# Where the split combinations of weight rows and of x are made in a two-layer fp32 decoder trunk

## Chip, cores and metric

The kernel runs on one core of one Trainium2 chip. The metric is the device time of one execution, in microseconds (us). Before the change the median of three runs is 2373.53 us (2373.14 to 2376.24).

## What is computed

The input x is 1024 tokens by 1024 features in fp32. Layer 0 is an mLSTM mixer, layer 1 attends in a window of 128 tokens to one shared K/V; each layer ends in a SwiGLU FFN of width 2816. Cut to what matters here:

```python
for l in range(2):
    x = x + mixer_l(rmsnorm(x, norm[l]))     # its last step is y @ w_out, y and w_out 1024 x 1024
    x = x + swiglu(rmsnorm(x, ffn_norm[l]), w_gate_up[l], w_down[l])
    if l == 0:
        k2, v2 = shared_kv(x, kv_norm, w_kv, b_kv)
return rmsnorm(x, final_norm)

def swiglu(x, w_gate_up, w_down):            # 1024 x 5632 and 2816 x 1024
    g, u = jnp.split(x @ w_gate_up, 2, axis=-1)
    return (jax.nn.silu(g) * u) @ w_down
```

## The kernel before, in words

**Seven products for eight.** Three matrix products of each layer, called out (y @ w_out), up (x @ w_gate_up) and down (hidden @ w_down), are made by a scheme with seven block products q = 0 to 6 in place of eight (`NQ = 7`). Each product needs one combination of the left blocks and one of the right blocks. Three of the seven are plain blocks, four are sums or differences (`SUM_A`, `SUM_B`). Every operand is then split in a high part (ScalarE, ACT, copies it to fp32r) and a low part (the source less the high part), and one product is three matmuls: high by high, high by low, low by high (L1939, L1940, L1941). A pair of split operands for one q is called a form here.

**Two sides.** The side that streams, `mats`, is remade for every item: sums by GpSimd (POOL, L918 to L923), high parts by ACT (L1100), low parts by VectorE (DVE, L1428) for plain q and by POOL (L928) for sums. The resident side, `forms`, has four slots of seven forms in SBUF, each form `[128, 2, 512]` fp32. In out and down a slot holds a row, that is 256 rows of w_out or w_down; in up the four slots hold the four quarters of the normed x.

**Items.** PE's work in a layer is a list of items, each seven products over `width` slots: 8 out items of width 2 (two chunks of two rows, four groups of tokens each), 22 up items of width 4 (one for each pair of 128 gate and 128 up columns), 16 down items (chunks of 3, 3, 3 and 2 rows of w_down, four groups each). Counted from the start of the layer they are items 0 to 7, 8 to 29 and 30 to 45. After each product of out or down DVE adds a 128x512 block of PSUM to X (L1446), and product 2 waits until the bank of product 0 is read, so an item is not quite free of DVE. PE, ACT, DVE and POOL each run a fixed program through the items, q by q, and wait for each other by semaphores; all loads and stores of this part are in SP's program, in order.

**Row forms.** Rows are loaded raw from w_out or w_down (1 MB each). Their four sums are made by POOL (`row_sum`, L900), their seven high parts by ACT (`row_hi`, L1090) and low parts by DVE (`row_lo`, L1422), inside the out and down items that precede their use. The first two rows of out and of down are made within item 0 and item 30 (`cold`), one row in item 29, the others one row in an item (`forms_after`).

**Seams.** The last chunk of out and of down is also a seam: as each group of X is done, ACT squares it (L1105), DVE scales the sum (L1476), POOL takes the power (L935), DVE norms the rows (L1488, for norm 2 L1485), and PE transposes them in the next item (L1957, L1968). For out the transposed group is split at once into the seven forms of its quarter (`quarter_hi`, `quarter_lo`: ACT L1116 and L1125, DVE L1498 to L1520, POOL L943). After item 7 the last quarter is transposed and split; then item 8 begins. X (4 MB) is parked in DRAM during the up part but for two tiles, its place being used for hidden blocks and raw rows, and is read back around items 29 and 30 (`x_reload`).

**Around the run.** Before layer 0's items lie four heads of the mLSTM (`head`), with the projections as plain three-pass products; after the last one DVE scales it and PE transposes it, and DVE gates it (`gate_head`) after item 0. PE's item 1 waits for that. Before layer 1's items lie the K/V and query projections and the attention steps.

Of the kernel before, what the change touches and what calls it, by code (L numbers as in the profile page):

```python
# [33 lines left out]
ALU = mybir.AluOpType  # L34
# [74 lines left out]
PLAIN_B = {0: (0, 0), 3: (1, 0), 5: (1, 1)}  # L109
SUM_B = {1: 0, 2: 1, 4: 2, 6: 3}  # L110


class Resident:


    def __init__(self, index, layer, part, number, slot):
        self.index, self.layer, self.part, self.number, self.slot = index, layer, part, number, slot
        self.slot_free_n = None
        self.before_in_raw = None
        self.before_in_sums = None  # L120


class Item:


    def __init__(self, n, kind, layer, width):
        self.n, self.kind, self.layer, self.width = n, kind, layer, width
        self.up = kind == "up"
        self.cold = False
        self.opens_chunk = False  # L130
        self.seam = None
        self.group = None
        self.rows = ()


class Unit:


    def __init__(self, base, turn=0):
# [4 lines left out]
        self.slot = base % RING  # L144
# [7 lines left out]
def yoco_kernel(nc, x, a_norm, a_w_in, a_b_gates, a_head_norm, a_w_out, kv_norm, w_kv, b_kv,  # L152
# [30 lines left out]
    forms_made, sums_made = [], []  # L183
    for l in range(2):
# [12 lines left out]
        out_rows = [add_row("out", p, p) for p in range(4)]  # L197
        for c in range(2):
            for g in range(4):
                it = add_item("out", 2)  # L200
                it.rows, it.group = out_rows[2 * c:2 * c + 2], g
                it.cold, it.opens_chunk = c == 0 and g == 0, g == 0
                it.seam = (1 + 2 * l, g) if c == 1 else None
# [5 lines left out]
        chunks = [down_rows[0:3], down_rows[3:6], down_rows[6:9], down_rows[9:11]]  # L209
        for c, chunk in enumerate(chunks):  # L210
            for i, g in enumerate((1, 2, 3, 0) if c == 0 else (0, 1, 2, 3)):
                it = add_item("down", len(chunk))
                it.rows, it.group, it.chunk = chunk, g, c
                it.cold, it.opens_chunk = c == 0 and i == 0, i == 0
                it.seam = (2 + 2 * l, i) if c == 3 else None
        for p, r in enumerate(down_rows):
            if p < 3:
                r.slot_free_n = last_up
            elif p == 3:
                r.slot_free_n = last_up  # L220
            else:
                r.slot_free_n = last_up + 4 * ((p - 4) // 3 + 1)
        p = down_rows
        out_rows[3].before_in_raw = out_rows[2]
        out_rows[3].before_in_sums = out_rows[2]
        p[1].before_in_sums = out_rows[3]
        p[2].before_in_sums = p[0]
        p[3].before_in_sums = p[1]
        for k in range(4, FP):
            p[k].before_in_raw = p[k].before_in_sums = p[k - 1]  # L230


        forms_made += [(r, q) for q in range(NQ) for r in out_rows[:2]]
        sums_made += [(r, k) for k in range(4) for r in out_rows[:2]]
        for r in out_rows[2:] + p[:1]:
            forms_made += [(r, q) for q in range(NQ)]
            sums_made += [(r, k) for k in range(4)]
        forms_made += [(r, q) for q in range(NQ) for r in p[1:3]]
        sums_made += [(r, k) for k in range(4) for r in p[1:3]]
        for r in p[3:]:  # L240
            forms_made += [(r, q) for q in range(NQ)]
            sums_made += [(r, k) for k in range(4)]

    form_no = {(r.index, q): i + 1 for i, (r, q) in enumerate(forms_made)}
    sum_no = {(r.index, k): i + 1 for i, (r, k) in enumerate(sums_made)}


    def forms_after(it, q):

        rr, i = run_rows[it.layer], it.n - runs[it.layer][0].n  # L250
        if it.cold and q < NQ:
            pair = rr[0:2] if it.kind == "out" else rr[5:7]
            return [(r, f) for f in ((0, 1, 2) if q < 0 else (q + 3,) if q < 4 else ()) for r in pair]
        if it.kind == "out":
            return [(rr[i], q)] if i in (2, 3) and q >= 0 else []
        if it.up:
            return [(rr[4], q)] if it.tile == FT - 1 and q >= 0 else []
        i -= 8 + FT
        c, g = i // 4, i % 4
        if c < 3 and g == 1 and q >= 0:  # L260
            return [(rr[4 + 3 * c + 3], q)]
        if c < 3 and g == 3 and q >= 0:
            return [(rr[4 + 3 * c + 4], q)]
        if c in (1, 2) and g == 0:
            third = rr[4 + 3 * c + 2]
            return [(third, f) for f in {-1: (0, 1, 2), 0: (3, 4), 1: (5, 6)}.get(q, ())]
        return []


    def refill_after(it, q):  # L270

        nxt = items[it.n + 1] if it.n + 1 < len(items) else None
        if nxt is None or nxt.layer != it.layer:
            return []
        if it.cold:
            return {5: [0, 1, 2], 6: [3, 4, 5, 6]}.get(q, [])
        if it.width == 2 and nxt.width == 4:
            return {1: [0], 3: [1], 5: [2]}.get(q, [])
        return [q]


    def refill_needs(it, q):

        before = items[it.n - 1]
        return NQ * before.n + (min(2 * q + 1, 6) if before.width == 2 and it.width == 4 else q) + 1
# [6 lines left out]
    seam_act = {1: 0, 2: 32, 3: 48}  # L292
    seam_dve = {1: 0, 2: 28, 3: 44}
    seam_pool = {1: 0, 3: 16}
    last_of_run = [runs[l][-1] for l in range(2)]
    sums_before = {0: {}, 1: {}}
    for l in range(2):
        r = run_rows[l]
# [1908 lines left out]
```

## Time and profile before

| | |
|---|---|
| median of the runs | 2373.53 us |
| the profiled execution | 2370.56 us, its span 2368.9 us |
| PE busy in the span | 2120.7 us (90%) |
| granted TensorE clock, mean | 0.946 |
| DMA traffic | 191.60 MB, mean 81 GB/s |

A window row gives a stretch of the span in us from its start, its length, the busy time of each engine with the count of its instructions, the granted clock as a share of full speed, the mean busy share of the 16 DMA engines and what they moved. Windows below begin where the first matmul of an item begins.

### The profile page before, as it was taken

To read this page: it belongs to the slowest core of one execution; us is meant where nothing else is said; L and a number is where in the kernel's file an instruction comes from. 1 tells how busy PE (TensorE), PEld (TensorE's weight loads), DVE (VectorE), ACT (ScalarE), POOL (GpSimd) and SP (SyncE) were. 2 spreads that over 40 slices of the span, in tenths; PEclk is the share of its full clock that TensorE was granted. 3 is DMA by queue.
4 is the path that set the end of the run, shared out by engine and by line. 5 is a ranking of instruction groups with operands and counts; after the bars stand their busy time and mean duration, and the time that the engine had idled before them with its cause. 6 is when DMAs were issued, how large, how long until landed. Compare 5 with 4: busy or idle time off the path is not lost.

```text
span 2368.9 us, 28393 instructions
## 1 busy us (share of the span) xinstructions
PE 2120.7 (90%) x9816; PEld 1731.4 (73%) x9816; DVE 1247.1 (53%) x2030; ACT 903.4 (38%) x1929; POOL 1271.5 (54%) x1009
## 2 busy tenths in 40 slices
PE   7999997659999999788979999875999999978896
PEld 6898895548888888566757777654788888857675
DVE  7433326753333334777764767776333333376775
ACT  5323323443333334333332544433433333333332
POOL 4222024766765555777736002376665666567873
PEclk9999999979999999899988999697999999989998
DMA  4222213213333222422212003122322222342222
GB/s 126 81 81 63 62 53 134 88 54 98 88 92 87 80 81 85 150 81 89 67 36 63 19 19 90 36 81 71 98 81 80 81 80 83 97 141 87 97 76 80
DMA packets 230867, 191.60 MB, mean 81 GB/s; under 512 B 31032, under 2 KB 209224, under 8 KB 230736
## 3 DMA queue, kind: packets, MB, share of 16 engines
q1 hardware_dynamic: 221824, 177.82, 25.1%
q10 hardware_dynamic: 7488, 7.34, 0.9%
q0 software_dynamic: 1424, 4.77, 0.6%
q8 instruction: 73, 1.20, 0.2%
q14 instruction: 58, 0.48, 0.1%
HBM read 147.93 MB, written 41.98 MB: 80 GB/s over the span
## 4 chain that ended last, share of the span: by engine, by line
PE 73%; DVE 12%; POOL 6%; issue 4%; ACT 4%; DMA 1%; SPq 0%; ACTq 0%; POOLq 0%; DVEq 0%
PE ps L1939 17%; PE ps L1940 17%; PE ps L1941 17%; PE ps L1840 7%; DVE forms L1422 4%; PE ps L1842 3%; DVE X L1446 2%; PE ps L2140 2%; POOL mats L928 1%; PE ps L2175 1%; PE ps L2177 1%; PE ps L2037 1%; PE ps L2036 1%; PE ps L2033 1%; POOL sum_b_s L900 1%
## 5 line engine op out<-in xcount | busy, mean ns | idle before, releaser
L1939 PE MATMUL ps<-forms,mats 128*128 128x512 f32 x2072 | 839.3, 405 | 167.9 <-DVE X L1446 110.1
L1940 PE MATMUL ps<-forms,mats 128*128 128x512 f32 x2072 | 827.5, 399 | 0.0
L1941 PE MATMUL ps<-forms,mats 128*128 128x512 f32 x2072 | 825.9, 399 | 0.0
L928 POOL TENSOR_TENSOR mats<-sum_a,mats 128x512 fp32r<-128x512 f32 (+2 forms) x368 | 425.6, 1164 | 473.8 <-ACT mats L1100 473.4
L1939 PEld LDWEIGHTS ps<-forms,mats 128*128 128x128 f32 x2072 | 402.0, 194 | 282.1 <-issue 178.0
L1941 PEld LDWEIGHTS ps<-forms,mats 128*128 128x128 f32 x2072 | 401.7, 194 | 87.0
L1940 PEld LDWEIGHTS ps<-forms,mats 128*128 128x128 f32 x2072 | 402.9, 194 | 82.2
L1100 ACT ACTIVATE mats<-sum_a 128x512 fp32r<-128x512 f32 (+2 forms) x368 | 199.9, 545 | 420.1 <-PE ps L1941 374.6
L1446 DVE TENSOR_TENSOR X<-ps,X 128x512 f32<-128x512 f32 x336 | 229.4, 685 | 158.2 <-PE ps L1941 158.0
L1428 DVE TENSOR_TENSOR mats<-stream_raw,mats 128x512 fp32r<-128x512 f32 (+2 forms) x276 | 248.1, 900 | 55.8 <-ACT mats L1100 54.5
L1100 ACT ACTIVATE mats<-stream_raw 128x512 fp32r<-128x512 f32 (+2 forms) x276 | 150.1, 544 | 284.6 <-PE ps L1941 247.8
L918 POOL TENSOR_TENSOR sum_a<-stream_raw 128x512 f32<-128x512 f32 (+2 forms) x92 | 104.6, 1137 | 262.8 <-DMA stream_raw<-scratch_y 187.9
L1840 PE MATMUL ps<-xT_hi,w_split 128*128 128x512 f32 x432 | 182.8, 423 | 3.1 <-issue 3.0
L1840 PE MATMUL ps<-xT_lo,w_split 128*128 128x512 f32 x432 | 170.7, 395 | 0.0
L1457 DVE TENSOR_TENSOR part<-ps,part 128x512 f32<-128x512 f32 x44 | 30.4, 692 | 257.6 <-PE ps L1941 257.4
L1842 PE MATMUL ps<-xT_hi,w_split 128*128 128x512 f32 x432 | 136.6, 395 | 0.0
L919 POOL TENSOR_TENSOR sum_a<-stream_raw 128x512 f32<-128x512 f32 (+2 forms) x92 | 130.5, 1419 | 0.0
L921 POOL TENSOR_TENSOR sum_a<-sum_a,stream_raw 128x512 f32<-128x512 f32 (+2 forms) x92 | 126.7, 1377 | 0.0
L1422 DVE TENSOR_TENSOR forms<-sum_b_s,forms 128x512 fp32r<-128x512 f32 x88 | 101.5, 1154 | 44.8 <-ACT forms L1090 44.2
L923 POOL TENSOR_TENSOR sum_a<-stream_raw,sum_a 128x512 f32<-128x512 f32 (+2 forms) x92 | 116.8, 1270 | 7.2
L868 POOL TENSOR_TENSOR raw<-raw,gain_cols 128x1024 f32<-128x1024 f32 x35 | 76.8, 2211 | 61.6 <-DMA raw<-in_a_w_in_dram 45.0
L1840 PEld LDWEIGHTS ps<-xT_hi,w_split 128*128 128x128 f32 x432 | 82.1, 190 | 33.6 <-issue 17.6
(216 smaller groups left out, 2715.0 us busy)
## 6 DMA issues: line engine op xcount, KB each, us to landing
stream_raw<-in_w_gate_up_dram SPq DMA_DIRECT2D x88, 512.0 KB, 5.2
scratch_hidden<-hidden SPq DMA_DIRECT2D x88, 256.0 KB, 5.3
stream_raw<-scratch_hidden SPq DMA_DIRECT2D x24, 768.0 KB, 4.8
resident_raw_e<-in_w_down_dram SPq DMA_DIRECT2D x32, 512.0 KB, 3.5
raw<-in_a_w_in_dram SPq DMA_DIRECT2D x24, 512.0 KB, 4.0
stream_raw<-scratch_y SPq DMA_DIRECT2D x16, 512.0 KB, 5.0
scratch_x<-X SPq DMA_DIRECT2D x12, 512.0 KB, 3.6
resident_raw_down<-in_w_down_dram SPq DMA_DIRECT2D x12, 512.0 KB, 5.3
```

Of the source, the lines that this page charges most:

```text
L919: pool.tensor_tensor(s[2], a11, a21, ALU.subtract)
L921: pool.tensor_tensor(s[1], s[0], a11, ALU.subtract).then_inc(ssum, 2)
L928: pool.tensor_tensor(blocks(m[:, q, 1, :], it.width), stream_source(it, q), blocks(m[:, q, 0, :].bitcast(F32), it.width), ALU.subtract).th ...
L1100: act.activation(blocks(mats[w][:, q, 0, :], w), stream_source(it, q), ACT.Copy).then_inc(hi_s, 1)
L1422: dve.tensor_tensor(forms[:, r.slot, q, 1, :], row_source(r, q), forms[:, r.slot, q, 0, :].bitcast(F32), ALU.subtract).then_inc(rlo, 1)
L1428: dve.tensor_tensor(blocks(m[:, q, 1, :], it.width), stream_source(it, q), blocks(m[:, q, 0, :].bitcast(F32), it.width), ALU.subtract).the ...
L1446: dve.tensor_tensor(xv, ps[:, s + BANK_OF[q], :], xv, ALU.add).then_inc(d_add, 1)
L1840: ms_ = [mm(ps[:, b + half, :], ah, t[:, c[half]], start=start and t is bh, stop=False) for half in halves for t in (bh, bl)]
L1842: ms_ += [mm(ps[:, b + half, :], al, bh[:, c[half]], start=False, stop=stop) for half in halves]
L1939: mm(dst, ah, bh, start=OPENS[q] and k == 0, stop=False, skip_group_check=True)
L1940: mm(dst, ah, bl, start=False, stop=False, skip_group_check=True)
L1941: m = mm(dst, al, bh, start=False, stop=k == w - 1, skip_group_check=True)
```

## The change

- Layer 0's four rows of w_out are split into forms one in each head: POOL makes four sums, ACT the high parts between its copies of v (`head_row_hi`), POOL the low parts, and POOL stores each form (512 KB) in a DRAM scratch, `scr_w` (`head_row`).
- The eleven rows of w_down of each layer, and in layer 0 also the four rows of w_out of layer 1, are split during up items 9 to 27 (`prep_rows`): in layer 0 105 forms over 133 steps (19 items of seven), in layer 1 77. POOL makes the sums, ACT the high part, DVE the low part, SP stores. There are two output buffers, so the high part of form k waits until form k-2 has landed in DRAM.
- Out and down items make no row forms. A row's seven forms are read from `scr_w`, issued on ACT's queue (the first two of each out part on SP's), as the products that used the slot before are done (`load_form`).
- Down has five chunks of 2, 3, 2, 2 and 2 rows, so 20 items a layer, with as many matmuls as before.
- In the seams ACT norms (`x_normed_of`), POOL scales and takes the power. For out the transposed tiles are only written to `xt` by DVE with the norm's gain (`evacuate`); the combinations for all four quarters are made after item 7, as item 8 needs them: POOL sums and low parts for two quarters, DVE for the other two, ACT all high parts.
- All eight tiles of X are parked. The streamed forms of item 0 are made in the last head and the last attention steps, and `gate_head` runs before item 0.

```diff
-        chunks = [down_rows[0:3], down_rows[3:6], down_rows[6:9], down_rows[9:11]]
-        for c, chunk in enumerate(chunks):
+        for c, width in enumerate((2, 3, 2, 2, 2)):
...
+        for r, at_item, free in zip(down_rows, (29, 29, 30, 31, 33, 34, 37, 38, 39, 42, 43),
+                                    (29, 29, 29, 29, 33, 33, 37, 37, 37, 41, 41)):
+            r.load_at, r.slot_free_n = at_item, runs[l][free].n
+        preps[l] += down_rows
+        if l == 1:
+            preps[0] += out_rows
...
+        events = [(runs[l][8 + f].n, q) for f in range(1, 20) for q in range(NQ)]
+        j0, forms_here = preps[l][0].prep, NQ * len(preps[l])
+        for k in range(forms_here):
+            prep_at.setdefault(events[k * len(events) // forms_here], []).append((j0 + k // NQ, k % NQ))
...
+            eng.dma_start(forms[:, r.slot, q].bitcast(F32), scr_w[r.layer, r.index % (4 + FP), q]).then_inc(row_in[q], 16)
...
+            def store_prep(j, q):
+                r, k = prep_rows[j], NQ * j + q
+                sp.wait_ge(prep_lo, k + 1)
+                sp.dma_start(scr_w[r.layer, r.index % (4 + FP), q], prep_out[k % 2][:].bitcast(F32)).then_inc(prep_stored[k % 2], 16)
...
                     if 9 <= i <= 30:
                         store_hidden(its[i - 1])
+                    if it.up:
+                        for q in range(NQ):
+                            for j, form in prep_at.get((it.n, q), []):
+                                store_prep(j, form)
+                                if form == NQ - 1 and j + 2 < end_prep:
+                                    load_prep(j + 2)
+                    if i == 28:
+                        for b in range(2):
+                            sp.wait_ge(prep_stored[b], staged(NQ * end_prep - 1, b))
+                        for t in (1, 5, 2, 6, 3, 7, 4):
+                            sp.dma_start(X[:, t, :], scr_x[l, t]).then_inc(x_back, 16)
...
+            def prep_hi_of(j, q):
+                k = NQ * j + q
+                if q in FORM_SUM:
+                    act.wait_ge(prep_sum, 4 * j + FORM_SUM[q])
+                else:
+                    act.wait_ge(prep_loaded[j % 2], raw_prep_at[j])
+                if k >= 2:
+                    act.wait_ge(prep_stored[k % 2], 16 * (k // 2))
+                act.activation(prep_out[k % 2][:, 0, :], split_source(prep_raw[j % 2], prep_t, q), ACT.Copy
+                               ).then_inc(prep_hi, 1)
...
+            def x_form_hi(l, q):
+                for c, g in enumerate(QUARTERS):
...
+                    act.activation(quarter(g, q, 0), x_form_source(g, q), ACT.Copy).then_inc(xf_hi, 1)
...
+            def x_form_lo(l, q):
+                for c, g in enumerate((2, 3)):
+                    pool.wait_ge(xf_hi, 28 * l + 4 * q + c + 1)
+                    pool.tensor_tensor(quarter(g, q, 1), x_form_source(g, q), quarter(g, q, 0).bitcast(F32),
+                                       ALU.subtract).then_inc(xf_lo_pool, 1)
...
                     if i == 7:
-                        quarter_lo(it.seam[0], 3, (0, 1, 2, 3))
-                        for q2 in (4, 5):
-                            stream_lo(its[i + 1], q2)
+                        for q in range(NQ):
+                            if q in SUM_B:
+                                x_form_sums(l, q)
+                            x_form_lo(l, q)
+                            if q in (3, 6):
+                                stream_lo(its[8], 4 if q == 3 else 5)
...
+            def x_normed_of(norm, i, t, e):
+                act.wait_ge(rstd_ready, norm * TT + 2 * i + e + 1)
...
+                act.activation((xp if norm == 2 else xn)[e][:], X[:, t, :], ACT.Copy, scale=rstd[:, t:t + 1]
+                               ).then_inc(xs_ready, 1)
...
-                    pe.wait_ge(rlo, max(form_no[r.index, q] for r in it.rows))
+                    pe.wait_ge(row_in[q], 16 * (it.rows[-1].index + 1))
                 if it.up and it.tile == 0:
...
+                    for done in (xf_lo_dve, xf_lo_pool):
+                        pe.wait_ge(done, 14 * l + 2 * q + 2)
```

## Rows read from the trace of the kernel before

**Rows 1.** The page's busy times over the whole span.
```profile
PE 2120.7 (90%) x9816; PEld 1731.4 (73%) x9816; DVE 1247.1 (53%) x2030; ACT 903.4 (38%) x1929; POOL 1271.5 (54%) x1009
```
**Rows 2.** Windows of layer 0: items 0-3, 4-7, 8, 9-28, 29, 30-45, after.
```profile
core 0: us, PE busy (x) PEld busy (x) DVE busy (x) ACT busy (x) POOL busy (x), PEclk, DMA share, GB/s
371.49:433.20 61.71, 45.23 (x171) 33.69 (x169) 49.49 (x69) 24.28 (x55) 44.48 (x43) 0.91 0.34 113
433.20:508.65 75.45, 50.98 (x213) 39.78 (x211) 48.06 (x69) 27.28 (x57) 46.43 (x45) 0.84 0.25 77
508.65:549.95 41.30, 26.25 (x106) 20.97 (x105) 17.71 (x24) 20.01 (x34) 26.78 (x21) 0.79 0.26 89
549.95:930.75 380.80, 380.80 (x1682) 315.31 (x1680) 134.25 (x160) 142.92 (x240) 234.73 (x165) 1.00 0.29 83
930.75:957.53 26.78, 19.20 (x86) 15.61 (x84) 19.76 (x21) 14.11 (x27) 15.15 (x13) 0.90 0.35 109
957.53:1227.40 269.87, 233.93 (x964) 184.72 (x964) 187.29 (x246) 98.23 (x193) 190.43 (x162) 0.94 0.27 88
1227.40:1245.00 17.60, 5.09 (x25) 3.95 (x25) 13.32 (x14) 7.48 (x13) 7.29 (x6) 0.64 0.07 30
```
**Rows 3.** Windows of layer 1: items 0-3, 4-7, 8, 29, 30-41, 42-45.
```profile
1512.42:1567.38 54.96, 43.70 (x169) 33.12 (x170) 47.33 (x65) 24.95 (x56) 44.97 (x44) 0.94 0.21 60
1567.38:1644.93 77.55, 53.08 (x213) 41.35 (x211) 47.92 (x69) 27.29 (x57) 46.34 (x45) 0.82 0.24 75
1644.93:1684.80 39.87, 24.85 (x107) 19.90 (x106) 17.93 (x24) 20.12 (x34) 27.25 (x21) 0.83 0.27 93
2065.59:2092.37 26.78, 19.20 (x85) 15.61 (x84) 19.76 (x21) 14.10 (x27) 15.14 (x13) 0.94 0.34 107
2092.37:2302.63 210.26, 186.00 (x756) 146.95 (x757) 152.60 (x185) 76.66 (x147) 167.30 (x133) 0.94 0.30 101
2302.63:2360.80 58.17, 44.83 (x169) 35.03 (x167) 32.79 (x52) 16.64 (x36) 26.37 (x30) 0.88 0.23 82
```
**Rows 4.** Windows of one item each, of width 4, 3 and 2, without row forms.
```profile
588.03:607.07 19.04, 19.04 (x85) 15.77 (x84) 7.24 (x8) 7.14 (x12) 16.89 (x13) 1.00 0.29 83
1070.34:1084.62 14.28, 14.28 (x64) 11.82 (x63) 7.83 (x11) 4.20 (x8) 9.84 (x10) 1.00 0.29 92
1528.55:1538.90 10.35, 9.80 (x43) 7.81 (x42) 7.07 (x11) 2.93 (x7) 5.17 (x8) 1.00 0.00 0
```
**Rows 5.** A window in which the DMA engines are never idle.
```profile
372.00:378.00 6.00, 3.53 (x15) 2.46 (x14) 6.00 (x8) 6.00 (x15) 5.02 (x6) 0.99 1.02 411
```
**Rows 6.** PE's waits in 371.5:523.6: who for whom, total us, times, longest.
```profile
PE ps L1939 <- DVE X L1446: 33.0, 12, 8.1
PE ps L1957 <- DVE x_normed_b L1488: 9.8, 1, 9.8
```
**Rows 7.** Groups: line engine op, names, shapes, count | busy us, mean ns | idle before.
```profile
L943 POOL TENSOR_TENSOR forms<-sum_x,forms 128x512 fp32r<-128x512 f32 x12 | 18.1, 1532 | 6.1 <-ACT forms L1125 6.1
L900 POOL TENSOR_TENSOR sum_b_s<-resident_raw_e,sum_b_s 128x512 f32<-128x512 f32 x16 | 24.4, 1526 | 1.4 <-POOL sum_b_s L900 1.4
L928 POOL TENSOR_TENSOR mats<-sum_a,mats 128x512 fp32r<-128x512 f32 x64 | 82.8, 1295 | 111.8 <-ACT mats L1100 111.8
L1422 DVE TENSOR_TENSOR forms<-sum_b_s,forms 128x512 fp32r<-128x512 f32 x36 | 41.9, 1163 | 19.8 <-ACT forms L1090 19.5
L1100 ACT ACTIVATE mats<-sum_a 128x512 fp32r<-128x512 f32 x64 | 40.2, 628 | 56.1 <-PE ps L1941 56.1
```
**Rows 8.** The timeline of DVE between norm 2 and the K/V projection.
```profile
1231.45 5.87 DVE L1485 TENSOR_SCALAR x_plain_a<-X,rstd 128x1024 f32<-128x1024 f32 x1
```
**Rows 9.** DMA issues: median us from issue to landing, of 512 KB each.
```profile
out_dram<-x_out SPq DMA_DIRECT2D x8, 512.0 KB, 2.6
scratch_x<-X SPq DMA_DIRECT2D x12, 512.0 KB, 3.6
X<-scratch_x SPq DMA_DIRECT2D x12, 512.0 KB, 6.3
```

More of the change, by code:

```diff
@@ L225, in yoco_kernel @@
[L225 to L267, printed above, removed]
@@ L270, in refill_after, with staged, last_slot_used @@
+    def staged(k, b):
+        return 16 * ((k + 1 - b) // 2 if k >= b else 0)
+    def last_slot_used(q, before, after):
+        return max(q, min(NQ - 1, ((q + 1) * after.width - 1) // before.width))
     def refill_after(it, q):
-        nxt = items[it.n + 1] if it.n + 1 < len(items) else None
-        if nxt is None or nxt.layer != it.layer:
+        i = it.n - runs[it.layer][0].n
+        if i + 1 == len(runs[it.layer]):
             return []
-        if it.cold:
-            return {5: [0, 1, 2], 6: [3, 4, 5, 6]}.get(q, [])
@@ L277, in refill_after @@
-        if it.width == 2 and nxt.width == 4:
-            return {1: [0], 3: [1], 5: [2]}.get(q, [])
-        return [q]
+        nxt = items[it.n + 1]
+        return [s for s in range(NQ if i != 7 else 3) if last_slot_used(s, it, nxt) == q]
     def refill_needs(it, q):
         before = items[it.n - 1]
-        return NQ * before.n + (min(2 * q + 1, 6) if before.width == 2 and it.width == 4 else q) + 1
+        return NQ * before.n + last_slot_used(q, before, it) + 1
     down_no = {it.n: m for m, it in enumerate(i for i in items if not i.up)}
@@ L312, in yoco_kernel @@
         stream_arrived[it.n] = stream_total[stream_buffer(it)]
-    def row_arrived(r):
-        if r.part == "out":
-            return (16, 48)[r.layer]
-        return 16 * (r.layer + 1)
     x2 = x[0]
@@ L1014, in _ @@
             load_rows_of_head(0)
-            for j in range(6, 11):
+            load_head_row(0)
+            for j in range(6, 8):
+                gain(Unit(U_HEADS + j))
+            head_row(0)
+            for j in range(8, 11):
                 gain(Unit(U_HEADS + j))
@@ L1202, in run @@
-                    if i == 7:
-                        quarter_hi(it.seam[0], 3, range(8))
-                        act.wait_ge(s_pool, 16 * (l + 1))
-                        for q in range(3, NQ):
-                            stream_hi(its[8], q)
+                        for r in rr:
+                            if r.load_at == i:
+                                if r.part == "out":
+                                    act.wait_ge(*x_free[l])
+                                else:
+                                    act.wait_ge(prod, NQ * r.slot_free_n + q + 1)
+                                load_form(act, r, q)
@@ L1312, in head @@
                     act.wait_ge(num_ready, h * TT + c + 1)
+                    if last and c:
+                        stream_hi(items[0], c - 1)
                     if c % 4 == 3:
@@ L1711, in head @@
                         write_lo(un[4 + c // 4] + LEAD)
+                    if last and c in (3, 6):
+                        stream_lo(items[0], c - 3)
                     i = 2 * c
@@ L1742, in _ @@
             head(NH_A - 1, NH_A - 1, False, last=True)
+            stream_lo(items[0], 6)
             scale_head(NH_A - 1)
+            gate_head(NH_A - 1, last=True)
             run(0)
```

727 lines of the change are left out of this document (341 added, 386 removed).

## Prediction, made before the changed kernel had run

> **What bounds the kernel now.** I read the page's busy times first. PE is busy 90% of the span and no other engine over 54% [rows 1], so only PE's idle time and its time at a low clock can be won. The windows say where these are. In items 9 to 28 PE is never idle and the clock is 1.00: 380.8 us for 20 items, 19.04 each [rows 2, 4]. The losses lie around them. In layer 0 items 0-3 take 61.7 us with 45.2 busy, items 4-7 75.5 with 51.0, item 8 with the wait before it 41.3, item 29 26.8 where a clean one takes 19.04, and items 30-45 269.9 [rows 2]; layer 1 has the same pattern [rows 3]. PE's waits name the cause: 33.0 us in the first out part is for DVE's add to X [rows 6]. The add itself is short; it stands in DVE's queue behind low parts of row forms (1163 ns each, [rows 7]), which wait for ACT and POOL. PE's other wait, 9.8 us, is for the norm of the last group.
>
> Clean items set the floor: width 4 19.04, width 3 14.28, width 2 10.35, the last with 9.8 of PE time [rows 4]. I take 10.3 for width 2.
>
> **Out part, items 0-7.** Removed are 28 row forms, each an ACT copy of 0.63 and a DVE operation of 1.16, and 16 POOL sums of 1.53 [rows 7]. In their place come 28 reads of 512 KB. Items 0-3 become 4 x 10.3 = 41.2. Item 4 is 10.3. Items 5-7 also carry 16 transposes each, about 2.1 us of PE, and the chain of two squares, scale and power, two norms on ACT (each of the four put at 1.1, just under twice the 0.63 of a copy half as wide, [rows 7]), transposes, `evacuate` at q=3. That chain reaches PE's second set of transposes about 0.8 us late, so 9.8 + 2.1 + 0.8 = 12.7 each, 38.1 for three. Bounds: 11.9 if the chain is hidden, 16.0 if it stays as bad as in layer 1's last items, (58.17 - 10.3)/3 [rows 3]. Together 89.6. Against 61.71 + 75.45 = 137.2 in layer 0 and 132.5 in layer 1 [rows 2, 3] that is -47.6 and -42.9. The reads of rows 2 and 3 (7.3 MB, 18 us at the 411 GB/s that a full DMA share moved [rows 5]) have 41 us and are hidden; without that cover they would cost item 4 what is late.
>
> **Start of the runs.** In layer 0 the last head now ends with one more high part and low part ahead of the head's scaling: +1.0 (0 to 2). `gate_head` moved ahead costs 2.7 us of DVE before the first add, but PE's first product takes 1.4 and its wait before item 1 goes, which is inside the 61.7. In layer 1 item 0 need no longer wait for forms: -2.2.
>
> **The forms of x, before and in item 8.** This step is dearer than before. After item 7's last product the last group needs 4.9 us until POOL can begin its first low part. POOL then has 8 sums and 14 low parts at 1.53 (the means of L900 and L943, [rows 7]) and two stream low parts of 1.3 (L928): 36.3. DVE has as many at 1.16, ACT 28 x 0.63 = 17.6, both less. So POOL sets the pace, about 5.2 us a form against PE's 2.7, and the seventh product ends at 4.9 + 36.3 + 2.8 = 44.0. The sums for item 9 come only then: 2.0 more. 46.0 against 41.30 and 39.87 [rows 2, 3]: +4.7 and +6.1. Bounds: all at the 1.30 of L928, -5; all a tenth dearer than 1.53 and the last products at the low clock, +9. PE idles in half of this, so I expect the low level (1.2 GHz) in part of it, as before (clock 0.79).
>
> **Up part, items 9-28.** Here work is added beside a PE that had no idle time. Per item of layer 0: 105/19 = 5.5 forms. ACT goes from 7.1 to 10.6, DVE from 6.7 to 13.1, POOL from 11.7 [rows 2] to about 18 (3.2 sums of 1.53, and about 1.5 for more overlap with DVE). All are below 19.04, POOL barely. What can bind is the pair of buffers: two forms take a high part 0.63, a low part 1.2, a store that lands after 2.6 [rows 9], the stores of out and 0.3 of semaphores, 4.7. That is 2.76 x 4.7 = 13.0 an item. The queue also carries the item's own 1.5 MB, 0.29 x 19.04 = 5.5 us of all DMA engines [rows 4], issued in one piece ahead of the stores, and 0.8 MB of raw rows, 2.0 us, mostly in gaps. Together 18.5 to 20.5; I take 19.8. What is late: ACT waits inside `prep_hi_of`, behind it its silu, then DVE's add for q=4, which PE's q=6 needs. So +0.8 x 19 = +15 (0 to +45). Layer 1 has 4.05 forms an item, 17.0 by the same sum: hidden, +3 for what POOL is behind after item 8 (0 to +10).
>
> The Trainium skill speaks against this term. Its page DMA: Bandwidth & Descriptors (Anatomy of one DMA) gives a DMA a fixed cost of about 2.0 us, mostly the receipt of the write, and HBM as the heaviest target; 512 KB is then 3.2 us, an estimate by that page. The trace has 2.6 for the same size and direction [rows 9], so I keep 2.6. By the page the item would be 21.5 and the layer's loss 46 in place of 15.
>
> **Item 29.** Its 7.7 us over the clean item was row forms that DVE made between its last add and item 30. Both layers: 2 x (26.78 - 19.04) = -15.5. The 14 reads for item 30 are released product by product, 1 MB in 2.6 us of DMA against 2.72 of PE, and have 16 us; hidden, but just.
>
> **Down part.** Layer 0: 4 items of width 3 57.1, 13 of width 2 133.9, three with transposes 38.1: 229.1 against 269.87, -40.8. More items of width 2 cost 0.8 each against their share of a width 3 item; that is in it. Layer 1: 57.1 + 12 x 10.3 = 123.6, and the last four as before, since DVE still does norm 4 and waits for POOL there: 58.2. 238.9 against 268.43: -29.5. Bounds: 9.8 to 11.0 for width 2, +-10 a layer. The late reads (one row, 3.7 MB, 9 us, for a window of 10 or 14) stand beside products.
>
> **After layer 0.** DVE's 5.87 us of x_plain_a [rows 8] stood beside three POOL operations and held PE; ACT now does it in about 1.1: -5.
>
> **Heads.** Four times 11 POOL operations and 9 DMA issues, put at 0.6 us each, lie in POOL's idle time (46% of the span, [rows 1]); one gain of a weight comes some 2 us later. +2 (0 to 8).
>
> **Sum.** -47.6 +1.0 +4.7 = -41.9 (out, layer 0); -42.9 -2.2 +6.1 = -39.0; -15.5; -40.8; -29.5; -5: -171.7. Against it +15 +3 +2. Net -151.7. PE's idle time in the windows that shrink is about 112 + 96 = 208 us, so there is room for it. Profiled 2370.56 - 151.7 = 2218.9; the median of before lies 3.0 above its profiled execution, so I forecast 2222, own range 2200 to 2245.
>
> **Rivals.**
> - *The store ring binds (22%).* Stores land as those of scratch_x did, after 3.6 [rows 9]: 2.76 us more an item, 19 x 2.76 = 52 in layer 0, layer 1 still at the edge. 2275. For it: the up part has no idle PE time, and its queue is shared. Against it: 3.6 was seen beside other transfers, which I count apart.
> - *The chains stay (13%).* Seam items stay at 16.0 (9 x 3.3 = 30) and POOL in the forms of x runs at 1.7 with a debt to the next items (about 18). 2270. For it: POOL is the pace there in any case.
> - *Reads come late (7%).* In items 29 to 31 four rows (14.7 MB, 36 us) and X (4.2 MB, 10 us) are read within about 40 us. If they queue, items 30 to 33 lose 15 a layer: 2252.
> - *Slower (6%).* The same ring, with stores that land after 6.3, as the reads of X did [rows 9]: 3.7 us more a pair of forms, 10.2 an item in layer 0 and 7.5, less 2.0 of slack, in layer 1, so 194 + 104 = 298: 2520. It decides from a landing of about 4.7 us on (2.1 more: 110 + 42 = 152). For it: 105 MB are written and as much read that were not before. Against it: the share is 0.29, and stores add 5.5 x 1.3 us an item, to about 0.77.
> - That rows were hidden anyway and the change brings nothing (2%): the waits of [rows 6] speak against it.
>
> **Numbers.** The forecast holds 50%, the rivals as said. Range 2190 to 2285: below it needs all bounds at their good ends, above it is the slower case and the worst of the ring. About 0.2% (4.7 us) is what a measurement tells from no change. Faster 0.92, same 0.02, slower 0.06.
>
> **What would show it.** Clean windows of about 10.3 and 14.28 in out and down, with no PE wait for DVE's add beyond 0.5. Item 8 with its wait at 46, PE waiting for POOL's low parts, POOL busy throughout. Items 9 to 27 of layer 0 at 19 to 20.5 with ACT waiting for a DMA to `scratch_forms`; layer 1 at 19.04. Item 29 at 19.04. The forecast is wrong if layer 0's up items are over 21, if out and down items of width 2 are over 11.5, or if PE waits for `forms<-scratch_forms`.

## The result: faster by 2.3%, where 6.4% was forecast

The changed kernel takes 2317.78 us (median of four runs, 2316.42 to 2323.76) beside 2374.89 for the kernel before: ratio 0.9765, interval 0.9745 to 0.9784. The gain is 57 us and not 152, and the time lies outside the range of 2190 to 2285. The profiled execution has a span of 2314.9 us.

The page's busy times, to be read beside [rows 1]:

```profile
PE 2099.2 (91%) x9816; PEld 1724.1 (74%) x9816; DVE 1341.7 (58%) x2046; ACT 934.6 (40%) x2001; POOL 1330.5 (57%) x1181
DMA packets 295431, 415.02 MB, mean 179 GB/s; under 512 B 40040, under 2 KB 218232, under 8 KB 295296
```

The windows: the heads; layer 0's items 0-7, the forms of x with item 8, items 9-28, item 29, the down part, what follows it up to layer 1; then layer 1's items 0-7, forms with item 8, items 9-28 and down part. They answer to [rows 2, 3].

```profile
66.00:396.40 330.40, 309.58 (x1756) 273.72 (x1755) 119.94 (x202) 106.58 (x220) 134.10 (x118) 0.96 0.39 134
396.40:495.32 98.92, 86.50 (x386) 69.25 (x384) 54.88 (x90) 35.18 (x71) 50.24 (x70) 0.94 0.59 205
495.32:556.65 61.33, 27.94 (x101) 21.93 (x101) 44.96 (x36) 29.60 (x50) 51.80 (x38) 0.69 0.20 69
556.65:1005.26 448.61, 405.02 (x1681) 327.93 (x1680) 271.45 (x265) 196.58 (x345) 326.55 (x221) 0.95 0.69 231
1005.26:1024.30 19.04, 19.04 (x85) 15.77 (x84) 5.44 (x8) 5.86 (x12) 7.36 (x10) 1.00 0.83 305
1024.30:1253.30 229.00, 219.65 (x973) 178.66 (x971) 132.74 (x210) 77.48 (x165) 127.47 (x163) 0.99 0.58 214
1253.30:1517.75 264.45, 248.66 (x1433) 194.17 (x1432) 176.10 (x610) 121.89 (x484) 51.95 (x35) 0.96 0.21 63
1517.75:1606.00 88.25, 84.97 (x384) 68.61 (x384) 53.85 (x88) 35.12 (x71) 50.25 (x70) 0.98 0.54 185
1606.00:1666.73 60.73, 27.74 (x102) 21.64 (x101) 44.75 (x36) 29.71 (x50) 52.28 (x38) 0.69 0.20 70
1666.73:2047.53 380.80, 380.80 (x1682) 315.32 (x1681) 250.94 (x237) 184.44 (x317) 307.46 (x205) 1.00 0.67 223
2066.57:2307.10 240.53, 220.14 (x925) 179.32 (x923) 133.87 (x205) 65.65 (x147) 132.14 (x163) 0.94 0.57 212
```

Set against the terms of the forecast, in us (a stretch after less the same stretch before):

| stretch | forecast | measured | off by |
|---|---|---|---|
| heads, with the start of the run | +3 | +24.9 | +21.9 |
| out items 0-7, layer 0 | -47.6 | -38.2 | +9.4 |
| out items 0-7, layer 1 | -42.9 | -44.2 | -1.3 |
| forms of x and item 8, both layers | +10.8 | +40.9 | +30.1 |
| up items 9-28, layer 0 | +15 | +67.8 | +52.8 |
| up items 9-28, layer 1 | +3 | 0.0 | -3 |
| item 29, both layers | -15.5 | -15.5 | 0 |
| down part, layer 0 / 1 | -40.8 / -29.5 | -40.9 / -27.9 | +1.5 |
| from layer 0's last item to layer 1 | -7.2 | -20.6 | -13.4 |
| sum | -151.7 | -53.7 | +98 |

What was to be saved came. What was to cost little cost 134 us: the up part of layer 0, item 8, the heads. The waits of TensorE name each place. First those of the heads, then of 396.4 to 556.65, then of items 9 to 28 of layer 0 with ACT's own wait behind them:

```profile
PE ps L2076 <- DVE C_state L1732: 10.6, 3, 5.1
PE ps L2051 <- ACT v_one L1298: 4.9, 2, 2.9
```
```profile
PE ps L1945 <- ACT part L1161: 24.6, 1, 24.6
PE ps L1945 <- DVE X L1473: 10.2, 3, 8.7
```
```profile
PE ps L1945 <- DVE part L1487: 43.6, 18, 4.9
ACT prep_forms L1098 <- DMA scratch_forms<-prep_forms: 104.0, 39, 7.3
```

In items 9 to 28 of layer 0 TensorE is idle for 43.6 us, and busy for 405.0 where the same work took 380.8: behind many of the stalls the granted clock is at its lower level (1.2 GHz) for some microseconds. 43.6 + 24.2 is the whole 67.8. The mean clock of 0.95 accounts for some 22 of the 24.2 (0.05 x 448.6).

### The profile page after: what moved, and what is told of

Read it like the earlier page. It is cut to its first block, busy times and chain, and to the rows that moved or that the text cites. A ratio compares the mean times of both kernels' runs of the same rounds, so it can differ in the third digit from the quotient of the medians.

```text
span 2314.9 us, 29195 instructions
## 1 busy us (share of the span) xinstructions
PE 2099.2 (91%) x9816; PEld 1724.1 (74%) x9816; DVE 1341.7 (58%) x2046; ACT 934.6 (40%) x2001; POOL 1330.5 (57%) x1181
## 3 DMA queue, kind: packets, MB, share of 16 engines
q1 hardware_dynamic: 254992, 286.90, 37.9%
## 4 chain that ended last, share of the span: by engine, by line
PE 65%; DVE 11%; DMA 9%; POOL 4%; issue 4%; ACT 4%; SPq 3%; ACTq 0%; POOLq 0%; DVEq 0%
PE ps L1945 15%; PE ps L1946 15%; PE ps L1947 15%; PE ps L1848 7%; DMA scratch_forms<-prep_forms 6%; PE ps L1850 3%; DVE mats L1453 2%; DMA scratch_hidden<-hidden 2%; PE ps L2128 1%; DVE hidden L1496 1%; SPq L673 1%; DVE prep_forms L1447 1%; PE ps L2163 1%; PE ps L2165 1%; ACT prep_forms L1098 1%
## 5 line engine op out<-in xcount | busy, mean ns | idle before, releaser
L874 POOL TENSOR_TENSOR mats<-sum_a,mats 128x256 fp32r<-128x256 f32 (+2 forms) x400 | 421.2, 1057 | 469.7 <-ACT mats L1119 468.9
L1119 ACT ACTIVATE mats<-sum_a 128x256 fp32r<-128x256 f32 (+2 forms) x400 | 206.2, 517 | 315.8 <-PE ps L1947 289.9
L1453 DVE TENSOR_TENSOR mats<-stream_raw,mats 128x256 fp32r<-128x256 f32 (+2 forms) x300 | 275.1, 919 | 61.7 <-ACT mats L1119 61.1
L1119 ACT ACTIVATE mats<-stream_raw 128x256 fp32r<-128x256 f32 (+2 forms) x300 | 155.3, 518 | 277.0 <-PE ps L1947 247.1
L1447 DVE TENSOR_TENSOR prep_forms<-prep_raw,prep_forms 128x512 fp32r<-128x512 f32 x130 | 158.7, 1222 | 140.0 <-ACT prep_forms L1098 140.0
L864 POOL TENSOR_TENSOR sum_a<-stream_raw 128x256 f32<-128x256 f32 (+2 forms) x100 | 110.7, 1107 | 224.4 <-DMA stream_raw<-scratch_y 194.0
L865 POOL TENSOR_TENSOR sum_a<-stream_raw 128x256 f32<-128x256 f32 (+2 forms) x100 | 125.0, 1250 | 0.0
L869 POOL TENSOR_TENSOR sum_a<-stream_raw,sum_a 128x256 f32<-128x256 f32 (+2 forms) x100 | 116.0, 1160 | 7.8
L867 POOL TENSOR_TENSOR sum_a<-sum_a,stream_raw 128x256 f32<-128x256 f32 (+2 forms) x100 | 119.6, 1196 | 0.0
L1421 DVE TENSOR_TENSOR w_split<-raw,w_split 128x1024 fp32r<-128x1024 f32 x35 | 55.1, 1590 | 100.9 <-ACT w_split L1075 100.9
L1098 ACT ACTIVATE prep_forms<-prep_raw 128x512 fp32r<-128x512 f32 x130 | 81.1, 624 | 71.6 <-DMA scratch_forms<-prep_forms 68.2
```

The lines of the kernel that those rows point to most:

```text
L865: pool.tensor_tensor(s[2], a11, a21, ALU.subtract)
L867: pool.tensor_tensor(s[1], s[0], a11, ALU.subtract).then_inc(ssum, 2)
L874: pool.tensor_tensor(blocks(m[:, q, 1, :], it.width), stream_source(it, q), blocks(m[:, q, 0, :].bitcast(F32), it.width), ALU.subtract).th ...
L1119: act.activation(blocks(mats[w][:, q, 0, :], w), stream_source(it, q), ACT.Copy).then_inc(hi_s, 1)
L1447: dve.tensor_tensor(dst[:, 1, :], split_source(prep_raw[j % 2], prep_t, q), dst[:, 0, :].bitcast(F32), ALU.subtract).then_inc(prep_lo, 1)
L1453: dve.tensor_tensor(blocks(m[:, q, 1, :], it.width), stream_source(it, q), blocks(m[:, q, 0, :].bitcast(F32), it.width), ALU.subtract).the ...
```

## The experiments

All are the changed kernel with the edits named. Their ratios are to the kernel before, whose median beside them was 2374 to 2376 us. The places that the first four edits change hardly touch, so each is also read by its own stretch.

**1. The order on GpSimd in the heads.**

```diff
-                for j in range(LEAD + 1, LEAD + 4):
+                for j in range(LEAD + 1, LEAD + 5):
                     gain(Unit(U_HEADS + j, h))
                 head_row(h)
-                for j in range(LEAD + 4, LEAD + 1 + RING):
+                for j in range(LEAD + 5, LEAD + 1 + RING):
```
(and the same for head 0)

> The changed kernel with one edit: in each head GpSimd scales the weights of the ninth unit (unit 8 of head 0, and the like in each head) before it makes the head's seven forms and not behind them. Theory A (the order on GpSimd costs the heads their 24.9 us: gain waits behind the forms, so ScalarE's and VectorE's halves of that unit come late and TensorE waits for the state C): the waits for C (10.6 us in 3 before) go, and the heads fall from 396.4 us by 12 to 20 us, so the time is 2298 to 2306 us, ratio to the kernel before 0.968 to 0.971. Theory B (the forms' own work on the shared engines, ScalarE's copies and VectorE's operations stretched beside GpSimd, costs it, in whatever order): the heads stay at 391 to 397 us, the time at 2312 to 2319 us.

Measured: 2302.86 us, ratio 0.9704 [0.9674, 0.9734]. The start of item 0 moves from 396.4 to 383.4 us, TensorE's wait for C from 10.6 to 1.8 us. Theory A. The prediction had this step ("one gain of a weight comes some 2 us later") and did not follow it to who waits: ScalarE's and VectorE's halves of the unit, C, TensorE. Of the 24.9 us this is 13.0; 11.9 stay, of them 6.6 a wait for `v_one` in head 0.

**2. The order on ScalarE in item 8.**

```diff
                             ...
                                     stream_hi(its[8], q2)
+                            if 2 <= q <= 4:
+                                up_out(its[8], q - 2)
```
(and item 8's own three calls go)

> The changed kernel with one edit: ScalarE's three copies for item 8 (which free TensorE's products 2, 4 and 5 of that item) stand between its copies for the forms of x, behind those of forms 2, 3 and 4, and not behind all 28. Theory A (the products of item 8 were held by the order on ScalarE, 24.6 us of waiting before product 2): that wait goes, and each layer's stretch from the end of item 7 to the end of item 8 falls from 61 us to 44 to 50 us, so the time is 2292 to 2306 us. Theory B (the forms themselves are made at that pace, by GpSimd and VectorE, and the wait only moves to products 5 and 6): each stretch stays at 56 to 61 us and the time at 2308 to 2318 us.

Measured: 2311.83 us, ratio 0.9732 [0.9712, 0.9752]. The wait of 24.6 us is gone, and item 8, counted from its own first product, fell only from 50.1 and 49.5 to 48.3 and 47.1: theory B in the main. TensorE now waits product by product for the forms.

```profile
506.41:554.72 48.31, 29.82 (x85) 21.73 (x85) 37.24 (x27) 21.86 (x39) 44.56 (x29) 0.75 0.19 65
```

GpSimd (44.6 us) and VectorE (37.2) are busy together. Here lies the lesson of this stretch: the largest wait in the view was not what the time hung on.

**3. A third buffer for the high halves.**

```diff
+                sp.wait_ge(prep_hi, k + 1)
+                sp.dma_start(dst[:, 0, :], prep_h[k % 3][:].bitcast(F32)).then_inc(hi_stored[k % 3], 16)
                 sp.wait_ge(prep_lo, k + 1)
-                sp.dma_start(scr_w[...], prep_out[k % 2][:].bitcast(F32)).then_inc(prep_stored[k % 2], 16)
+                sp.dma_start(dst[:, 1, :], prep_l[k % 2][:].bitcast(F32)).then_inc(lo_stored[k % 2], 16)
```

> The changed kernel with one edit in the up part: a form's high half and low half are stored by transfers of their own (256 KB each, twice as many transfers), the high halves from three buffers and the low halves from two, and ScalarE waits only for the store of the high half three forms back. Theory A (the ring of two buffers, each held by copy, subtraction, issue and landing, sets the pace where layer 0 makes 105 forms in 19 items): layer 0's items 9 to 28 fall from 448.6 us to 381 to 400 us, layer 1's stay at 380.8, and the time is 2250 to 2272 us, ratio 0.947 to 0.957. Theory B (the bytes stored, or ScalarE's and VectorE's extra operations, set it): items 9 to 28 stay above 430 us and the time at 2300 us or more; the doubled number of transfers could even add some us.

Measured: 2301.42 us, ratio 0.9676 [0.965, 0.9703]; items 9 to 28 of layer 0 take 426.95 us, between the two theories; the time is in theory B's range. The window; then, from 577 to 965 us, DVE's and ACT's waits for the stores, and the DMA issues with their landings:

```profile
556.77:983.72 426.95, 395.06 (x1682) 320.90 (x1681) 269.97 (x265) 196.55 (x345) 326.11 (x221) 0.98 0.74 243
```
```profile
DVE prep_lo L1460 <- DMA scratch_forms<-prep_lo: 52.9, 18, 7.6
ACT prep_hi L1109 <- DMA scratch_forms<-prep_hi: 13.9, 7, 3.7
```
```profile
scratch_forms<-prep_hi SPq DMA_DIRECT2D x100, 256.0 KB, 4.4
scratch_forms<-prep_lo SPq DMA_DIRECT2D x99, 256.0 KB, 3.5
```

Half the bytes land no sooner (these are medians). ScalarE's wait fell from 104.0 us to 13.9, and VectorE took over with 52.9: the low halves still have two buffers. A whole form landed in 3.5 (median) in the changed kernel.

**4. The row loads one item later.**

```diff
-        for r, at_item in zip(out_rows[2:], (0, 1)):
+        for r, at_item in zip(out_rows[2:], (1, 2)):
...
-        for r, at_item, free in zip(down_rows, (29, 29, 30, 31, 33, ...
+        for r, at_item, free in zip(down_rows, (29, 29, 31, 32, 33, ...
```

> The changed kernel with one edit: the loads of the forms of the second pair of rows are issued one item later, in items 1 and 2 of each layer for the out part (were 0 and 1), in items 31 and 32 for rows 2 and 3 of the down part (were 30 and 31). Theory A (in items 1 and 32 TensorE waits for VectorE, which waits for a stream that lands late behind those 3.5 MB of form reads): the waits in items 1 and 32 (8.7, 5.8 and 7.7 us) shrink by more than half, and the time is 2302 to 2311 us. Theory B (the first rows' own reads, 7 MB issued before, fill the engines then, or the stream waits for something else): no more than 3 us, 2314 to 2320 us; if the second pair then comes late for items 4 and 34, new waits there and a longer time.

Measured: 2291.13 us, ratio 0.9653 [0.9626, 0.968], better than theory A. Item 1 of layer 0 after the change, then the same item here, then item 32 of the two layers here (17.55 and 20.10 us before the edit):

```profile
407.70:427.96 20.26, 11.55 (x43) 9.14 (x42) 6.36 (x10) 2.92 (x7) 6.04 (x9) 0.75 0.93 346
```
```profile
407.61:417.18 9.57, 9.57 (x43) 7.88 (x42) 6.22 (x10) 2.93 (x7) 6.08 (x9) 1.00 0.91 312
1032.08:1041.60 9.52, 9.52 (x43) 7.88 (x42) 6.07 (x10) 2.93 (x7) 6.07 (x9) 1.00 1.02 415
2066.82:2076.34 9.52, 9.52 (x44) 7.88 (x43) 6.07 (x10) 2.93 (x7) 6.07 (x9) 1.00 1.02 417
```

The three items give 29.3 us; items 33 behind them give 1.4 and 2.0 back, and 26.7 us lie between the medians. The DMA share is no lower here, 0.91 to 1.02: the engines are full, only what waits is something else. What was late, in the changed kernel from 396 to 430 us:

```profile
POOL sum_a L864 <- DMA stream_raw<-scratch_y: 11.8, 1, 11.8
ACT mats L1119 <- DMA stream_raw<-scratch_y: 11.2, 1, 11.2
```

That stream landed 17.0 us after its issue there, and 8.1 here. At item 32 of layer 0 a small store was late too: the last hidden block landed 17.4 us after its issue, and 7.9 here. SyncE waits for that store before it reads the last tile of X, and the stream of item 33 stands behind both in its program. This is the rival "reads come late" in a place the prediction did not name: it is not the rows that are late but the small transfers beside them.

**5. The item's own transfers in another queue.**

```diff
+                        if q == 0 and 9 <= i <= 27:
+                            stream_used(it, act)
+                            load_stream(its[i + 2], act)
+                        if q == 1 and 9 <= i <= 30:
+                            store_hidden(its[i - 1], act)
                         for j, form in prep_at.get((it.n, q), []):
+                            if form == 0 and preps[l][0].prep < j < preps[l][-1].prep:
+                                act.wait_ge(prep_lo, NQ * j)
+                                load_prep(j + 1, act)
                             prep_hi_of(j, form)
```
(and SyncE issues these no longer)

> The changed kernel with one edit in the up part: the item's own transfers (stream of item i+2, the two halves of hidden, the raw rows) are issued by ScalarE, so that SyncE's queue carries only the stores of the forms; the ring of two buffers stays. Theory A1 (a store is late because it stands in one queue behind the 1.5 to 2.5 MB that the item issues in a piece; with three high buffers layer 0's items 9 to 28 still took 427.0 us): stores land in 3.0 us or less, and items 9 to 28 of layer 0 fall from 448.6 us to 381 to 410 us; time 2256 to 2287 us. Theory A2 (the 16 engines share their time over all queues, so that which queue it is doesn't matter): 435 to 455 us, time 2305 to 2325 us. Theory C (the pace is VectorE's and GpSimd's, whose operations of 512 elements take 1.7 to 1.8 us side by side): no change either, and VectorE's idle time stays as it is.

Measured: 2284.23 us, ratio 0.9624 [0.961, 0.9639]. Items 9 to 28 of layer 0:

```profile
556.25:982.09 425.84, 396.40 (x1681) 320.52 (x1680) 276.13 (x265) 196.71 (x345) 327.86 (x221) 0.98 0.71 243
```
```profile
scratch_forms<-prep_forms SPq DMA_DIRECT2D x105, 512.0 KB, 3.9
```

That is -22.8, but neither theory: the stretch lies between A1's and A2's, and the landing that A1 wanted shorter did not fall. Worked out from the trace, form by form, the mean time from the start of one high part to that of the next in the same buffer, in us:

| part of the cycle | layer 0, changed | layer 1, changed | layer 0, run 5 |
|---|---|---|---|
| high part (ACT) | 0.63 | 0.62 | 0.63 |
| until the low part begins | 0.66 | 0.49 | 0.46 |
| low part (DVE) | 1.19 | 1.32 | 1.17 |
| until the store is issued | 0.53 | 0.23 | 0.03 |
| issue to landing | 4.07 | 4.06 | 4.02 |
| until the next high part | 1.12 | 2.67 | 1.42 |
| two forms | 8.18 | 9.39 | 7.73 |

SyncE, which no longer stands in other waits, issues a store 0.5 us sooner. That it lands no sooner leaves the shared time of the 16 engines as the likely reason for 4 us; no run took that apart.

The edit also had a price. From 557 to 983 us:

```profile
ACT prep_forms L1094 <- issue: 37.9, 26, 4.7
PE ps L1949 <- DVE part L1491: 16.7, 12, 2.8
PE ps L1949 <- ACT part L1165: 12.7, 9, 2.9
```

ScalarE now stands 37.9 us before high parts with nothing to wait for that the profile shows ("issue"); the changed kernel has no such row in this stretch, and the likely reason is the transfers that ScalarE now issues and waits to issue. Of TensorE's 29.4 us of waiting 12.7 are for ScalarE's copies, where all 43.6 were for VectorE. So the edit took waiting from one queue and put some into another, and the 22.8 us are what is left of it.

The other effect was not expected: items 32 fell to 9.52 in both layers, some 18.6 us. The hidden's stores are now issued by ScalarE and land 10.3 us after their issue in place of 17.4 (layer 0), so SyncE issues the stream behind them sooner.

**6. All forms of x on VectorE** (with edit 2).

```diff
-                for c, g in enumerate((0, 1)):
-                    dve.wait_ge(xf_hi, 28 * l + 4 * q + c + 3)
+                for k, g in enumerate(QUARTERS):
+                    dve.wait_ge(xf_hi, 28 * l + 4 * q + k + 1)
```
(the same in the sums; GpSimd's are taken out)

> The changed kernel with the copies of item 8 between (as in the run before) and GpSimd's half of the forms of x (8 sums, 14 low parts a layer) given to VectorE, which then does all 16 sums and 28 low parts. Theory D (side by side the two engines take 1.72 us for an operation that VectorE does in 0.69 alone, so that they take turns and VectorE alone is as fast as both): item 8 falls from 48.3 and 47.1 us to 36 to 44 us, VectorE's operations take 0.7 us; time 2300 to 2310 us. Theory E (VectorE is slow there for another reason, its sources or its waits for ScalarE, and two engines are worth their number): item 8 rises to 60 us or more, time 2325 us or more.

Measured: 2291.48 us, ratio 0.9664 [0.9646, 0.9681]. Item 8 takes 36.9 and 38.5 us. Theory D. One engine does in less time what two did: its 44 operations take 28.3 us from the first to the last, where the two together take 41.9 in run 2 (from the trace). Two of VectorE's groups in item 8 of layer 0 in run 2, where GpSimd works beside it; then from this run the window of item 8, the same group, and GpSimd's timeline (start, length):

```profile
L1530 DVE TENSOR_TENSOR sum_t<-x_transposed,sum_t 128x512 f32<-128x512 f32 x2 | 3.5, 1772 | 0.0
L1489 DVE TENSOR_TENSOR part<-ps,part 128x512 f32<-128x512 f32 x1 | 0.7, 683 | 0.0
```
```profile
507.13:544.06 36.93, 25.01 (x85) 19.00 (x85) 30.76 (x47) 23.09 (x40) 24.00 (x9) 0.79 0.23 79
```
```profile
L1527 DVE TENSOR_TENSOR sum_t<-x_transposed,sum_t 128x512 f32<-128x512 f32 x4 | 2.5, 681 | 0.0
```
```profile
518.60 12.43 POOL L874 TENSOR_TENSOR mats<-sum_a,mats 128x512 fp32r<-128x512 f32 x1 [18.89 <-ACT mats L1115]
```

The same sum takes 1772 ns beside GpSimd and 681 alone; an addition with one source in PSUM takes 683 beside it. And the one operation that GpSimd had to do while VectorE ran without a pause took 12.43 us, while VectorE's beside it still took 0.68: here GpSimd bore the whole wait, and in run 2 both did. Why they share it so differently, no run shows. The Trainium skill says of this (SBUF — State Buffer, Who interferes with whom) that a VectorE instruction with two inputs in SBUF contends with a GpSimd one that reads SBUF, and one with a single input there does not; the 1772 and the 683 ns agree.

**7. Four edits at once** (1, 2, 4 and 5).

> The changed kernel with four edits at once: gain of the ninth unit first, copies of item 8 between, row loads one item later, and the item's own transfers on ScalarE's queue. The first three gave -13, -4.5 (item 8 of both layers) and -29 us in their own places. If they add up and the queue is worth 40 to 65 us: 2205 to 2235 us, ratio 0.929 to 0.942. If the queue is worth nothing: 2268 to 2278 us.

Measured: 2253.06 us, ratio 0.9503 [0.9488, 0.9518], between the two: the heads give 13.2, items 1 and 32 28.7 in place of 29.3, the queue 22.8 in layer 0 and nothing more, since items 32 can be won but once. Items 33 and 34 of layer 1 take 5.6 us more than in the changed kernel.

**8. 105 forms in layer 1 too.**

```diff
-        preps[l] += down_rows
+        preps[l] += (down_rows[:4] if l == 1 else []) + down_rows
```

> The changed kernel, but layer 1 makes 105 forms in its 19 up items as layer 0 does, and not 77: its first four down rows are made and stored twice. Theory A (the count of forms against the ring's pace decides, nothing else of layer 0): layer 1's items 9 to 28 rise from 380.8 us to 435 to 460 us and the time by as much, 2370 to 2395 us. Theory F (layer 0 is slow for a reason of its own, such as what the heads or its loads left behind): below 400 us in layer 1, time below 2340 us.

Measured, a single execution: 2373.42 us. Layer 1's items 9 to 28 with 105 forms:

```profile
1664.19:2105.29 441.10, 399.33 (x1682) 323.51 (x1680) 272.75 (x265) 196.90 (x345) 332.69 (x221) 0.96 0.69 235
```

Theory A: 60.3 us more in layer 1 for 28 forms, and nothing for the 77 before them. The loss has an edge. 77 forms leave 9.4 us for two, 105 forms 2 x 133 x 2.72 / 105 = 6.9, and the buffers need 7.1 (8.18 less the 1.12 of waiting), before any unevenness. The mean alone doesn't place the edge: by the same count run 5 needs 6.3 (7.73 less 1.42) of its 6.9, and its layer 0 still takes 45 us too long. Landings spread widely, with a median of 3.5 and a tenth of them above 6.0 us in the changed kernel, and ScalarE and VectorE come late on their own account.

**9. Both remedies for the ring**, with edits 1, 2, 4 and 6, and ScalarE's copies of head 0's forms behind the values of the head.

> The kernel of four edits with three more: three high buffers and two low ones with stores of their own (beside the queues apart), all forms of x on VectorE, and in head 0 ScalarE's copies for the head's forms placed behind the values of the head (they held TensorE for 6.6 us there). Theory A (the ring's period: in the changed kernel two forms took 8.18 us on average, of which the landing was 4.07 and the buffer's wait 1.12; the need is 6.9 with none to spare, so that either edit alone took only half of the 67.8 us): together items 9 to 28 of layer 0 fall to 381 to 400 us from 425.8 (queues alone) and 427.0 (buffers alone). Item 8 gives 10 a layer, head 0 some 5. Time 2198 to 2218 us, ratio 0.926 to 0.934. Theory C (what is left, 45 us, is VectorE's and GpSimd's work side by side): items 9 to 28 stay at 415 to 426 us and the time at 2220 to 2235 us.

Measured: 2216.6 us, ratio 0.9342 [0.9329, 0.9354]: the fastest here, 101 us below the changed kernel. Items 9 to 28 of layer 0:

```profile
519.37:929.51 410.14, 389.79 (x1681) 316.02 (x1680) 277.56 (x265) 194.52 (x345) 331.30 (x223) 0.99 0.76 253
```
```profile
DVE prep_lo L1465 <- DMA scratch_forms<-prep_lo: 58.0, 28, 5.5
```

The remedies add up in the main, -38.5 of the 67.8, and miss theory A's 400 by 10. VectorE still waits 58.0 us for a store of a low half. A third buffer for those wasn't tried, and ScalarE's row "issue" is 55.3 us here, so that the 29 us that are left are not taken apart. The edit in head 0 brought nothing: item 0 begins at 383.5 us as in run 1, and the wait for `v_one` fell to 1.6 us but one of 5.5 for C came in the same head. The stretch from item 30 to layer 1 is 7.8 us longer than in run 7, 7.0 of it in the attention steps, whose code no edit touches: over the twelve profiles they take 201.0 to 202.7 us in eight, 206.9 to 208.0 in three, and 212.8 in the kernel before.

**10. The sums for row forms on VectorE** (with all of 9).

```diff
+                            if form == NQ - 1 and j < preps[l][-1].prep:
+                                prep_sums(j + 1, (1, 2, 3))
```
(in VectorE's program, with the calls for sum 4 and the first row; out of GpSimd's)

> As the run before, and in the up part the sums for the row forms (4 a row, 60 in layer 0 and 44 in layer 1) are VectorE's and no longer GpSimd's. Theory D (where both engines work at once an operation of 512 elements takes each 1.7 us against VectorE's 0.62 to 0.69 alone, so that work taken from GpSimd frees more of VectorE's time than it costs): layer 0's items 9 to 28 no longer than in the run before, or up to 10 us shorter. Theory E (VectorE is nearly full there and paces the low parts): 10 to 30 us longer, with TensorE waiting for VectorE's additions.

Measured: 2240.49 us, ratio 0.9444 [0.9429, 0.9458]. Theory E: layer 0's items 9 to 28 take 423.9 us, 13.8 more, layer 1's 385.4, 4.5 more.

```profile
520.99:944.89 423.90, 392.86 (x1682) 318.35 (x1680) 286.83 (x325) 193.67 (x345) 238.13 (x163) 0.98 0.73 245
```

GpSimd is busy 93 us less, and VectorE, with 60 operations more, only 9 us more, so the two do free each other. But the sums now stand ahead of the low parts and additions that TensorE waits for. What holds in item 8, where all of the work is one chain, doesn't hold where the order of the queue decides.

## Why the prediction was wrong, step by step

- **What bounds the kernel, out and down parts, item 29: right but for one step.** Width 2 takes 9.5 us and not 10.3, so that four clean items give 3 us more than put down; in the down parts that made up for the late streams of item 32; in layer 0's out part the late stream of item 1 (10.7 us, run 4) showed. "The reads of rows 2 and 3 ... are hidden" is that step: they are, but the streams beside them are not. The bytes were right; that a load in no hurry can stand ahead of one that is awaited was not looked at.
- **The store ring: the mechanism right, the landing mis-sized.** The sum had 4.7 us for two forms with a landing of 2.6 and added the shares of the other traffic as if they ran in turn: 19.8 us an item. Measured are 8.18 for two forms, 22.6 an item, of it 4.07 for the landing. The 2.6 is the median of the stores in the last four items, where the DMA share was 0.23 [rows 3]; the like median here is 3.5, and the mean 4.07. The row beside it, 3.6 for the store of X [rows 9], was made the first rival at 22%. Its 22.6 an item and 52 us more in layer 0 are what came, but that they fit to the decimal is luck. For two forms the rival had 3.6 of landing, 2.5 of other traffic in turn and 0.3 for semaphores; the trace has 4.07 of landing, the other traffic in it, and 2.3 until SyncE, VectorE or ScalarE came: 6.4 either way. The Trainium skill's page DMA: Bandwidth & Descriptors (Anatomy of one DMA), by which an item would take 21.5 (an estimate), was nearer than the row I kept; its figures are for transfers that GpSimd issues, and these stores are SyncE's. Layer 1 was hidden whole, and run 8 finds the edge between 77 and 105 forms. Had this rival been all, the time would have been 2275, inside the range; the heads and item 8 made the rest.
- **The forms of x: failed, in two places.** "POOL then has 8 sums and 14 low parts at 1.53", "DVE has as many at 1.16": side by side GpSimd's take 1.6 to 1.7 each and VectorE's 1.2 to 1.8, and they also wait for each other and for ScalarE. And the products were taken to follow the forms, "about 5.2 us a form": they could not, for ScalarE's program held product 2 behind all 28 copies. Undoing the order alone gave 2 us a layer; undoing the sharing as well gave 11 and 9 more (runs 2 and 6).
- **The heads: failed.** POOL's idle share said that 11 operations and 9 issues fit. They do, but not where they were put. 13.0 us is the place of one gain (run 1); of the 11.9 left a part is the first head's wait, and the rest was not taken apart.
- **After layer 0: -20.6 for -7.2.** The tail of norm 2 gives 6.6, the K/V projection 0.7, layer 1's start 3.1, and the attention steps 10.2. Before, GpSimd's sums for layer 1's out rows stood beside VectorE in the last steps, where the granted clock was 0.77 for 49 us; after it is 1.00 there. Since those steps vary by 6 us between kernels that share their code (run 9), not all of it is shown to be the change's.
- **The range** took in the worse ring, but for the heads (0 to 8) and the forms of x (up to +9) only durations: no bound had an order in a queue in it, and these two came 52 us above their terms together.

## What to carry to other kernels

Work given to an engine with idle time is free only if nothing that a critical engine needs stands behind it in the queue: for each insertion, name the next instruction behind it and follow it to TensorE. Price a ring of buffers by a landing that was measured while other traffic ran, and compare its period with the time that each form has. Two engines that both read SBUF may be no faster than one.

## What the runs showed of the hardware that was not expected

- VectorE alone does the 44 operations of 128x512 with both sources in SBUF in 28 us, VectorE and GpSimd together in 41 to 42; and GpSimd's one operation beside them took 12.43 us (12.44 in layer 1), while some twenty of VectorE's went by.
- Beside other traffic 256 KB lands no sooner than 512 KB (medians of 3.5 and 4.4 us against 3.5), and a queue of its own doesn't make the landing shorter (median 3.9, mean 4.02 against 4.07).
- Many of the stalls of 2 to 5 us are followed by the lower clock: in layer 0's up items TensorE is busy 24.2 us longer beside 43.6 of waiting, at a mean granted clock of 0.95; in run 9 it waits 20.3 us and the mean is 0.99.
- With the DMA engines at a share of 1.02 TensorE ran items of width 2 in 9.52 us at full clock: full engines cost these items nothing, as the small transfers that they need had gone first.
